# A group's query sums in one run behind its query product, in a two-layer streaming encoder on one core

## The reference

```python
def rmsnorm(x, gain):
    y = x * rsqrt(mean(x * x, axis=-1, keepdims=True) + EPS)
    return y * gain

def window_attention(hn, w_qkv, q_gain, k_gain, sinks, w_o, real_queries_only):
    q, k, v = split(hn @ w_qkv)
    q = rmsnorm(q.reshape(..., N_KV_HEADS, Q_PER_KV, HEAD_DIM), q_gain) * HEAD_DIM ** -0.5
    k = rmsnorm(k.reshape(..., N_KV_HEADS, HEAD_DIM), k_gain)
    s_band = q . k over the two chunks, minus slope * distance
    s_meta = q . k over the 16 meta keys
    probs  = softmax over [s_meta, s_band, sink]
    out    = probs @ v
    return out @ w_o
```

## Time and profile before

| | |
|---|---|
| median of 3 runs | 1940.2 us |
| the three runs | 1940.20, 1939.62, 1940.31 us |
| the profiled execution, its own time | 1938.08 us |
| span of its trace | 1936.3 us |
| TensorE matmuls busy | 1922.4 us, 99% |
| TensorE weight loads busy | 1808.8 us, 93% |
| VectorE busy | 959.7 us, 50% |
| ScalarE busy | 605.2 us, 31% |
| GpSimd busy | 317.6 us, 16% |

### The profile page before, as it was taken

How to read it: one execution, slowest core, us unless ns; L and a number is a source line. 1 busy time by engine, 2 the same in 40 slices (tenths; PEclk the granted TensorE clock), 3 DMA queues, 4 the chain that set the end, 5 groups by cost and what they waited for, 6 DMA issues and landing times.

```text
span 1936.3 us, 33860 instructions
## 1 busy us (share of the span) xinstructions
PE 1922.4 (99%) x13943; PEld 1808.8 (93%) x13943; DVE 959.7 (50%) x1063; ACT 605.2 (31%) x711; POOL 317.6 (16%) x568
## 2 busy tenths in 40 slices
PE   8999999999999999999999999999999999999999
PEld 8999999999999999999999999999878778888887
DVE  5443367566765444344564443445556654434443
ACT  5222222332243222222332222223355432222222
POOL 2888889011230000000000000000011000000000
PEclk9999999999999999999999999999999999999999
DMA  6322544444333322422243223332411143333323
GB/s 178 88 83 83 150 135 149 129 129 131 96 88 88 87 81 82 114 83 81 68 122 87 81 82 105 82 88 69 122 44 45 45 109 87 88 86 108 103 70 88
DMA packets 329042, 185.61 MB, mean 96 GB/s; under 512 B 7304, under 2 KB 322984, under 8 KB 328968
## 3 DMA queue, kind: packets, MB, share of 16 engines
q1 hardware_dynamic: 323296, 166.81, 30.9%
q0 software_dynamic: 5344, 17.69, 3.2%
q10 hardware_dynamic: 328, 0.07, 0.0%
HBM read 173.56 MB, written 9.80 MB: 95 GB/s over the span
## 4 chain that ended last, share of the span: by engine, by line
PE 98%; DVE 1%; ACT 0%; DMA 0%; issue 0%; SPq 0%
PE ps L737 78%; PE ps L975 5%; PE ps L1017 2%; PE ps L1072 2%; PE ps L1036 1%; PE ps L1168 1%; PE ps L1203 1%; PE ps L1135 1%; PE ps L1137 1%; PE ps L1113 1%; PE ps L1124 0%; PE ps L782 0%; PE ps L910 0%; PE ps L936 0%; PE ps L935 0%; PE ps L926 0%
## 5 line engine op out<-in xcount | busy, mean ns | idle before, releaser
L737 PE MATMUL ps<-xl,wh 128*128 128x264 f32 (+1 forms) x2432 | 564.1, 301 | 0.0
L737 PE MATMUL ps<-xh,wh 128*128 128x264 f32 (+1 forms) x2432 | 563.0, 301 | 0.1
L737 PE MATMUL ps<-xh,wl 128*128 128x264 f32 (+1 forms) x2432 | 562.7, 301 | 0.0
L1508 DVE TENSOR_TENSOR wl<-raw,wh 128x2048 fp32r<-128x2048 f32 x172 | 407.6, 2370 | 171.8 <-ACT wh L1214 171.6
L737 PEld LDWEIGHTS ps<-xh,wh 128*128 128x128 f32 x2432 | 389.9, 188 | 17.1 <-issue 0.7
L1214 ACT ACTIVATE wh<-raw 128x2048 fp32r<-128x2048 f32 x172 | 327.7, 1905 | 246.7 <-PE ps L737 211.3
L737 PEld LDWEIGHTS ps<-xl,wh 128*128 128x128 f32 x2432 | 388.9, 188 | 15.5 <-issue 0.2
L737 PEld LDWEIGHTS ps<-xh,wl 128*128 128x128 f32 x2432 | 388.6, 189 | 15.0
L737 PE MATMUL ps<-act_l,wh 128*128 128x264 f32 (+1 forms) x1232 | 284.8, 301 | 0.0
L737 PE MATMUL ps<-act_h,wh 128*128 128x264 f32 (+1 forms) x1232 | 284.8, 301 | 0.0
L737 PE MATMUL ps<-act_h,wl 128*128 128x264 f32 (+1 forms) x1232 | 284.5, 301 | 0.0
(11 more groups left out here) (304 smaller groups left out, 1740.7 us busy)
## 6 DMA issues: line engine op xcount, KB each, us to landing
raw<-in_ff_w_gate SPq DMA_DIRECT2D x88, 512.0 KB, 4.0
raw<-in_ff_w_up SPq DMA_DIRECT2D x87, 512.0 KB, 5.2
raw<-in_ff_w_down SPq DMA_DIRECT2D x64, 384.0 KB, 4.0
raw<-in_ff_w_down SPq DMA_DIRECT2D x64, 320.0 KB, 3.7
raw<-in_even_w_in SPq DMA_DIRECT2D x16, 512.0 KB, 5.3
raw<-in_attn_w_qkv SPq DMA_DIRECT2D x12, 512.0 KB, 4.7
raw<-in_even_w_out SPq DMA_DIRECT2D x8, 512.0 KB, 4.8
raw<-in_attn_w_o SPq DMA_DIRECT2D x8, 512.0 KB, 4.8
```

Source lines behind the costliest of these rows:

```text
L737: last = nc.tensor.matmul(ps[:, 2 * pair + hf, 0:nh], w[:, slot, b * P:(b + 1) * P], x[:, k0 + k, c0 + hf * nh:c0 + (hf + 1) * nh], start= ...
L1508: v.tensor_tensor(wl[:, c % 2, :], raw[:, c % 2, :], wh[:, c % 2, :].bitcast(F32), ALU.subtract).then_inc(wl_ready, 1)
```

## The change

The sums of a group are no longer made in pieces behind each block of the product beside them. The call moves out of the loop over blocks, and all eight stand in one run behind the last block. In the units n = 0 and n = 4 that is behind four blocks of `query_part`, instead of two products behind each; in n = 8 behind two blocks of `out_part`, instead of four products behind each. The first of the eight waits, and the last signals, as before.

```diff
@@ query_part
                     for q, (w, x) in enumerate(((wh, xh), (wh, xl), (wl, xh))):
                         last = nc.tensor.matmul(ps[:, 2 + t, :], w[:, slot, b * P:(b + 1) * P], x[:, k, c0:c0 + width],
                                                 start=(k == 0 and q == 0), stop=(k == KD - 1 and q == 2))
-                    if sums is not None:
-                        at = 2 * (k - half * KD // 2)
-                        query_sums(sums, at, at + 2)
+                if sums is not None:
+                    query_sums(sums)
                 if half:
                     last.then_inc(tile_full, 1)
@@ out_part
                     for q, (w, x) in enumerate(((wh, act_h), (wh, act_l), (wl, act_h))):
                         last = nc.tensor.matmul(ps[:, 2 + d, :], w[:, (WO[0] + d // 2) % 2, b * P:(b + 1) * P], x[:, k, c0:c0 + width],
                                                 start=(k == 0 and q == 0), stop=(k == KD - 1 and q == 2))
-                    if sums is not None:
-                        query_sums(sums, NT * (k - k0), NT * (k - k0 + 1))
+                if sums is not None:
+                    query_sums(sums)
                 return last
```

## The result

The changed kernel takes 1942.61 us (median), the kernel before 1939.61 us in the same series. The ratio is 1.0015, with a 95% interval of 1.0008 to 1.0021: slower by 3.0 us. That is under the 0.2% that the prediction took as its bound, so "no change" in that sense holds, but the interval leaves out 1, and the median lies 0.8 us above the range. The profiled execution took 1942.25 us with a span of 1940.5, against 1938.08 and 1936.3. Each kernel had 22 executions, of which one ran in a slow state (2324.7 and 2327.88 us) and is left out of the ratio.

The account below looks back on a forecast made before the run. TensorE's instruction stream was taken to bound the kernel (99% busy). Group terms of +0.04, +0.03 and +0.01 us summed to +0.08, added to the 1940.2 us median: 1940.3 us, range 1938.8 to 1941.8.

Parts of the forecast that it names:

- the range: Whole kernel: forecast time between 1938.8 and 1941.8 us.
- the three stretches: Groups 1, 2 and 3, first wide matmul to value product: +0.04, +0.03 and +0.01 us against now.
- the cheaper run: Seven inner switches of groups 1 to 3: 0.09 us saved at each, 0.6 us faster, 1939.6; chance 0.08.
- the exposed loads: Seven pairs or fours lose the wide matmul over their first load: 0.8 us slower, 1941.0; chance 0.05.
- the late sums: Scores of the next group wait if the last pass is late beyond 1.8 us of cover: slower; chance 0.01.
- No change within 0.2%: Whole kernel: the moved sums add +0.08 us, under the measurable 0.2% or 3.9 us; chance 0.84.
- the third rival, the falling clock: TensorE's clock falls in the 1.7 us of narrow passes, slowing wide work behind: 1944.2 or more; chance 0.02.
- the sum: Changes of the stretches of groups 1, 2 and 3 added up: +0.08 us in all.
- Its rule on weight loads: TensorE pulls loads ahead, so a pair now costs next to nothing; set aside for the trace's 0.45 us.

Follow-up runs that it names:

- e1: Changed kernel with each run of eight sums moved to the middle of its product, wide matmuls on both sides; ratio 1.0002, median 1939.68 us.
- e8: Groups 1 and 2 in one run behind the third block of four, group 3 as in the kernel before; ratio 0.9999 against the kernel before.
- e17: Changed kernel with group 1's run behind its second block, groups 2 and 3 as in the change; ratio 1.0000 against the kernel before.
- e3: Only the `query_part` hunk of the change (groups 1 and 2), group 3 as in the kernel before; ratio 1.0017 against the kernel before.
- e10: Kernel before with the whole run for group 1 alone (unit 0), other groups as before; ratio 1.0016.
- e5: Changed kernel with the sums of groups 1, 2 and 3 made twice in a row; 1954.98 us, ratio 1.0081 against the kernel before.
- e6: Kernel before with the sums of groups 1, 2 and 3 made twice, still split between blocks; 1947.64 us, ratio 1.0040.
- e13: e10 with five spare wide matmuls filling the idle time in front of unit 0's scores; ratio 1.0014 against the kernel before.
- e18: The changed kernel measured once more, unaltered, on the same chip as e17; ratio 1.0009 against the kernel before.
- e4: Only the `out_part` hunk of the change (group 3), groups 1 and 2 as in the kernel before; ratio 1.0000 against the kernel before.
- e7: Kernel before with group 0's run of eight sums moved behind the first block of the next query product; ratio 0.9999, mean 1939.50 us.
- e9: Groups 1 and 2 as four products behind the second and four behind the fourth block, group 3 as before; ratio 1.0005 against the kernel before.
- e11: Kernel before with the whole run for group 2 alone (unit 4), other groups as before; ratio 1.0002.
- e12: e1 with group 0's run also behind a block as in e7; median 1938.19 us, ratio 0.9997 against the kernel before.
- e16: The same kernel as e12, measured in a second series; median 1938.61 us, ratio 0.9997 against the kernel before.
- e15: Kernel before with TensorE made to wait for unit 5's exponentials in front of unit 4's scores; ratio 1.0033.

## Why the prediction was wrong

**What held.** TensorE bounds the kernel. A pass costs 0.11 us wherever it stands: the run was put at 1.71 us and took 1.71, and the three stretches were put at 4.60, 4.60 and 3.18 and took 4.57, 4.57 and 3.17. No wait came or went; the cheaper run, the exposed loads and the late sums did not happen. "No change within 0.2%" holds for the ratio, but by the width of that bound and not by the mechanism: 3.0 us were lost where 0.1 was forecast.

**What failed is the third rival, the falling clock.** Its cost stood at nothing in the sum and in the upper end of the range; it was priced only from 3.9 us upward, as falls behind all three runs, and the fall behind group 1's run alone cost 2.96 us. (The base of the sum was 0.6 us high, 1940.2 against 1939.61 in the series of the result; the change itself was forecast at 0.1 us and measured at 3.0.) The rival was given 0.02, mainly on one piece of evidence: that group 0's run, as long and at a clock of 1.00, stood in the profiled execution. That was one execution of the best class. Of the 17 profiles in which group 0's run stands where it did, nine have the clock low from about its end on, those of the change and of e1 among them. The prediction noticed that the profiled execution was 2.1 us under the median and carried the difference along as a constant; it was at least in part the mark of a lower clock that this execution did not have: the classes lie at 1937.80, 1939.56 and 1940.33, the profiled one at 1938.08 and the three runs shown at 1939.62 to 1940.31. Read as classes, they would have said that a clock of 1.00 in this execution says little about the others.

**The place was wrong too.** The rival looked at the 1.7 us of passes by themselves. What counts is the run together with the value products, scores and transposes behind it: 4.80 us from the first pass to the next wide matmul (unit 4 at the full clock, 1471.29 to 1476.09), where the kernel before had 3.45 (unit 0, 1442.96 to 1446.41). Shown by e1, e8 and e17 (the same run with a wide block behind it: 1.0002, 0.9999, 1.0000) against e3 and e10 (1.0017, 1.0016), and by e5 against e6. The clocks say the same. Group 1's run stands in front of the value products in six of the 20 profiles (the change, e3, e5, e10, e13, e18), and in five of these the clock is low in units 0 and 1, for 6.8 us in four and for 3.4 in e3; in the other 14 it never is. Over the executions, 39 of 65 are at 0.996 with the run there (the change in both series, e3, e10, e13), 2 of 99 without (e1, e4, e7, e8, e9, e11, e12, e16, e17), and none of the 137 of the kernel before.

**A rule that was read as cover.** The prediction held that the clock falls only where TensorE has gaps. The trace differs: it fell at 1445.7, with no gap in TensorE's order since the scores at 1438.49. So the sentence of the Trainium skill that the prediction leaned on ("TensorE: Matmul & The Clock Gate", "The HAM clock gate"), which names idle time as what brings the clock down, does not cover this case. Its rule on weight loads (same page, "Architectural detail") was rightly put aside: the passes cost the same in both orders.

**What stays open.** Why group 1 pays and group 2 does not, with the same order of TensorE's work from the four blocks in front of the run to the next query product. The fall is rarer there: behind group 2's run the clock is low in two of the seven profiles that have it in front of the value products (e5, with doubled sums, and e11), against five of six. And it can be shorter: 3.4 us in e11 (1.46 us more from value product to value product than the 6.07 of the kernel before, 1469.74 to 1477.27) against 6.8 in e10 (2.98 us more, 1445.45 to 1454.50); but in e3 it was 3.4 us behind group 1's run too. What makes it rarer or shorter isn't known; it isn't the 1.1 us idle time in front of unit 0 (e13). What else stands in front of the four blocks differs, and was not tried: a query product in unit 0, the value products of unit 3 in unit 4. Nor is it known what decides in which executions the clock falls, nor whether the gain of e12 and e16 is real.

```profile
1445.45 0.47 PE L1137 MATMUL ps<-arena 128*128 128x128 f32 x2
...
1454.50 0.38 PE L1137 MATMUL ps<-arena 128*128 128x128 f32 x2
```

```profile
1469.74 0.47 PE L1137 MATMUL ps<-arena 128*128 128x128 f32 x2
...
1477.27 0.38 PE L1137 MATMUL ps<-arena 128*128 128x128 f32 x2
```

## What to carry to other kernels

Two orders of the same matmuls can cost the same to 0.01 us in the sum and still differ by 3 us, through the clock of what follows: keep narrow products apart, with a block of wide ones between them, even where no load is hidden by it. Here only one place of three paid, so try each by itself. A profiled execution that is faster than the median of its kernel is evidence about itself alone; compare its time and granted clock with those of the other runs before it is used to rule a rival out.

## What the runs showed of the hardware

- The clock can fall to the low level with TensorE without a gap, behind narrow work: at 0.50 for 6.8 us in units 0 and 1 of the changed kernel, and there in five of the six profiles with group 1's run in front of the value products, in none of the other 14.
- It does so in some executions of a program and not in others: the changed kernel's profile has the clock low from about the end of group 0's run on, that of e18, the same program, has not; over 17 profiles with this run in its place it is nine. By its mean clock the kernel before has three classes of time, 1937.80, 1939.56 and 1940.33 us at the median, with 53, 43 and 41 of 137 executions.
- 2.1 us of idle time in front of narrow work cost more than itself: medians of 1943.81 in e15 against 1939.25 us in the kernel before, 4.6 us for a wait of 2.1, with the clock low for 6.8 us from the wait on in its profile.
